# Order of the last two experts, of their last weights and of the tiles' norm, and the first expert's turn, on one Trainium2 core

## The chip, the cores and the metric

One core of a Trainium2 chip runs one launch. The metric is the device time of that launch in microseconds. The engines are TensorE (PE), VectorE (DVE), ScalarE (ACT), GpSimd (POOL) and SyncE (SP), whose queue issues most of the loads and stores.

## The reference, cut to what matters

Two transformer blocks run one after the other on 1024 tokens of width 1024, in float32. The change touches the last part of the second block, the mixture of 16 experts and the norm behind it:

```python
def expert_choice_moe(h, w_router, w_gate, w_up, w_down):
    cap = CAPACITY_FACTOR * T // N_EXPERTS            # 128 tokens for each expert
    gate, idx = lax.top_k(jnp.swapaxes(affinity, 1, 2), cap)
    xe = jax.vmap(lambda hb, ib: hb[ib])(h, idx)
    a = jnp.einsum('becd,edf->becf', xe, w_gate)      # each weight 1024 x 1024
    u = jnp.einsum('becd,edf->becf', xe, w_up)
    ye = jnp.einsum('becf,efd->becd', jax.nn.silu(a) * u, w_down) * gate[..., None]
    # combine: out[idx] += ye
...
x = x + g2 * expert_choice_moe(hx2, ...)
return rmsnorm(x, final_norm_g)
```

## The kernel before, in words

All engines run their own list of instructions, written out by hand in order; they meet at semaphores. `x.did(name, key)` counts an event, `x.wait_ge(name, key)` waits for it.

**Weights.** The 16 experts have 48 matrices, cut into 192 weights of 256 rows by 1024 columns (1 MB), numbered n in the order in which TensorE uses them (`EW`, `moe_order`, L3609). SP loads weight n into one of eleven places (`e_load`), once the weight eleven before is split. ScalarE rounds it to float32r, the high part (`e_high`), once the weight four before is used up, as there are four pairs of places for high and low parts. VectorE subtracts to get the low part, the rest (`e_low`). TensorE makes each float32 product of three float32r matmuls: high by high, high by low, low by high (`mm3`, L411). One weight (k index 0 and 1, column halves c of 512) is 12 matmuls, in two groups of six.

**An expert e.** TensorE does the gate product (gate e), the up product, the turn of the next expert's tokens (`turn_x`, 8 transposes), the down product of the expert before (down e-1), and the turn of the hidden row (`turn_h`, 8 transposes). ScalarE applies silu to the gate; VectorE multiplies it with up into `hb` (events `eu_out`, one for each half). After a turn ScalarE rounds (`xe_high`, `hb_high`) and VectorE subtracts (`xe_low`, `hb_low`). VectorE scales the down product into `yt`; GpSimd scatters it with an add into `xa_dram` (event `sc_st`), and gathers the tokens for the experts ahead.

**The end.** In expert 15 the order is gate 15, down 14, up 15, `turn_h` 15, down 15. The tokens of expert 15 are not scattered. When scatter 14 has landed, SP reads back `xa_dram` as eight tiles `XF[i]`, and GpSimd gathers the 128 rows of expert 15 (`rows`). ScalarE squares and sums each tile, VectorE forms mean and inverse root with ScalarE's root between them, scales the tiles (`y_out_f`) and SP stores them. `last_rows(c)` (L3934) adds half c of down 15 to `rows`; then `rows` has its own norm, and GpSimd writes these rows over the stored tiles, last of all.

**Queues around the change.** TensorE waits for the low part of each weight, in the order of the weights. In `moe_act` (L3817) and `moe_dve` (L3839) each product brings four roundings and four rests for the weights three to six ahead of its first, and then the product's own work (silu, `hb`, `yt`).

## Time and profile before

| what | value |
|---|---|
| median of 3 runs | 2835.88 us (2834.59 to 2837.06) |
| the profiled execution | 2833.19 us |
| its span | 2831.4 us |
| busy: PE, DVE, ACT, POOL | 2728.4, 2013.1, 1312.0, 555.9 us |
| experts, first transpose to the last matmul | about 2248 to 2812 us |
| end of the span behind the last matmul | 19 us |

Times in the rows are us from the span's start. A row of the timeline has the start, the length, the engine, the line and operation, what is written and read, how many instructions are merged into it, and in brackets how long the engine sat idle before it and what ended that. Matmul ends are modelled and overlap the next one's start, so a group's length over its count is the pace. L132 is any matmul, L135 any transpose, L138 any activation, L141 any `tensor_tensor`, L147 any `scalar_tensor_tensor`; shapes tell them apart: 128x2048 is a weight, 128x1024 a tile, 128x512 half a tile or a turned half.

### The profile page before, as it was taken

To read this page: it belongs to the slowest core of one execution; us is meant where nothing else is said; L and a number is where in the kernel's file an instruction comes from. 1 tells how busy PE (TensorE), PEld (TensorE's weight loads), DVE (VectorE), ACT (ScalarE), POOL (GpSimd) and SP (SyncE) were. 2 spreads that over 40 slices of the span, in tenths; PEclk is the share of its full clock that TensorE was granted. 3 is DMA by queue.
4 is the path that set the end of the run, shared out by engine and by line. 5 is a ranking of instruction groups with operands and counts; after the bars stand their busy time and mean duration, and the time that the engine had idled before them with its cause. 6 is when DMAs were issued, how large, how long until landed. Compare 5 with 4: busy or idle time off the path is not lost.

```text
span 2831.4 us, 35182 instructions
## 1 busy us (share of the span) xinstructions
PE 2728.4 (96%) x13692; PEld 2186.4 (77%) x13692; DVE 2013.1 (71%) x2776; ACT 1312.0 (46%) x2035; POOL 555.9 (20%) x499
## 2 busy tenths in 40 slices
PE   7999999999999999999999999999999399999996
PEld 6777778788778888988888876666788288888885
DVE  5344455888885788787866656665665689999997
ACT  4344534333332455433222355454323277777775
POOL 0011111655455011511111121111100300100000
PEclk9999999999999999999999999999999699999998
DMA  4110123445552997233222260111763699999996
GB/s 151 51 46 31 45 77 110 123 123 160 177 169 68 381 282 218 79 101 111 83 82 74 106 193 31 45 38 38 219 217 144 233 362 396 395 397 396 396 396 234
DMA packets 270617, 494.11 MB, mean 175 GB/s; under 512 B 30124, under 2 KB 141892, under 8 KB 269940
## 3 DMA queue, kind: packets, MB, share of 16 engines
q1 hardware_dynamic: 240864, 396.40, 40.2%
q0 software_dynamic: 29440, 95.43, 10.5%
q8 instruction: 109, 1.79, 0.3%
q14 instruction: 56, 0.46, 0.1%
q10 hardware_dynamic: 148, 0.04, 0.0%
HBM read 424.60 MB, written 67.21 MB: 174 GB/s over the span
## 4 chain that ended last, share of the span: by engine, by line
PE 87%; DVE 6%; ACT 2%; DMA 2%; issue 2%; POOL 1%; POOLq 0%; SPq 0%; DVEq 0%; ACTq 0%
PE PS L132 81%; PE PS L135 6%; DVE m L141 3%; ACT m L138 1%; DVE m L147 1%; POOL m L141 1%; DMA x_scratch<-m 1%; DVE m L183 0%; DVE m L186 0%; DVE m L180 0%; DMA m<-x_scratch 0%; ACT L138 0%; DVE m L150 0%; DMA m<-pc_scratch 0%; DMA m<-in_x_dram 0%
## 5 line engine op out<-in xcount | busy, mean ns | idle before, releaser
L132 PE MATMUL PS<-m,m 128*128 128x512 f32 (+6 forms) x11818 | 2526.8, 388 | 20.1 <-DVE m L141 10.3
L132 PEld LDWEIGHTS PS<-m,m 128*128 128x128 f32 (+2 forms) x11818 | 1987.8, 184 | 495.0 <-issue 90.6
L138 ACT ACTIVATE m<-m 128x512 fp32r<-128x512 f32 (+5 forms) x893 | 811.7, 930 | 877.1 <-PE PS L132 386.0
L141 DVE TENSOR_TENSOR m<-m,m 128x512 fp32r<-128x512 f32 (+5 forms) x920 | 1024.8, 1143 | 218.1 <-ACT m L138 199.6
L138 ACT ACTIVATE m<-PS 128x512 f32<-128x512 f32 (+3 forms) x497 | 276.9, 582 | 482.4 <-PE PS L135 288.7
L141 DVE TENSOR_TENSOR m<-PS,m 128x512 f32<-128x512 f32 (+1 forms) x456 | 300.1, 684 | 193.0 <-PE PS L132 136.7
L141 POOL TENSOR_TENSOR m<-m,m 128x512 f32<-128x512 f32 (+4 forms) x176 | 273.4, 1557 | 598.6 <-DVE m L141 260.0
L135 PE MATMUL PS<-ident,m 128*128 128x128 f32 x1650 | 230.7, 278 | 63.0 <-DVE m L156 36.0
L135 PEld LDWEIGHTS PS<-ident,m 128*128 128x128 f32 x1650 | 188.0, 141 | 111.8 <-DVE m L156 36.3
L138 ACT ACTIVATE m<-m,small 128x640 f32<-128x640 f32 (+4 forms) x200 | 156.1, 785 | 84.9 <-DVE small L150 84.6
L156 DVE COPY m<-PS 128x512 f32<-128x512 f32 (+2 forms) x160 | 97.1, 609 | 114.4 <-PE PS L135 87.4
L147 DVE SCALAR_TENSOR_TENSOR m<-m,small,m 128x512 f32<-128x512 f32 (+1 forms) x154 | 163.8, 1088 | 7.1 <-DMA m<-x_scratch 3.7
L150 DVE CUSTOM_DVE_ANT_0 m<-PS,m,small 128x640 f32<-128x640 f32 (+1 forms) x128 | 103.7, 847 | 63.4 <-PE PS L132 63.3
L147 DVE SCALAR_TENSOR_TENSOR m<-m,vecT,m 128x512 fp32r<-128x512 f32 (+3 forms) x96 | 63.4, 716 | 53.4 <-ACT m L138 52.8
L141 POOL TENSOR_TENSOR m<-m 128x512 f32<-128x512 f32 x62 | 85.2, 1382 | 29.7 <-DMA m<-in_w_gate_up_dram 17.5
L141 POOL TENSOR_TENSOR m<-ident,small 128x1024 f32<-128x1024 f32 x16 | 30.3, 1892 | 260.0 <-DVE small L162 260.0
L150 DVE CUSTOM_DVE_ANT_0 m<-PS,m 128x1024 f32<-128x1024 f32 (+7 forms) x64 | 45.8, 754 | 49.3 <-PE PS L132 49.3
L195 POOL DMA_INDIRECT m<-xh_scratch,small x16 | 20.2, 1264 | 300.0 <-PE PS L135 258.5
L141 DVE TENSOR_TENSOR m<-m,PS 128x512 f32<-128x512 f32 x75 | 50.8, 685 | 31.3 <-PE PS L132 31.2
L195 POOL DMA_INDIRECT xa_scratch<-m,small x15 | 25.6, 1709 | 216.7 <-DVE m L147 216.7
L138 ACT ACTIVATE m<-m,vecT 128x512 fp32r<-128x512 f32 (+2 forms) x80 | 41.2, 601 | 44.3 <-PE PS L132 44.3
L141 DVE TENSOR_TENSOR m<-m 128x512 f32<-128x512 f32 (+1 forms) x57 | 40.7, 714 | 0.1
(89 smaller groups left out, 495.8 us busy)
## 6 DMA issues: line engine op xcount, KB each, us to landing
m<-in_w_exp_gate_dram SPq DMA_DIRECT2D x64, 1024.0 KB, 8.1
m<-in_w_exp_up_dram SPq DMA_DIRECT2D x64, 1024.0 KB, 8.5
m<-in_w_exp_down_dram SPq DMA_DIRECT2D x64, 1024.0 KB, 7.7
m<-in_w_mod_dram SPq DMA_DIRECT2D x48, 512.0 KB, 3.7
m<-in_w_gate_up_dram SPq DMA_DIRECT2D x44, 512.0 KB, 6.4
m<-in_w_in_dram SPq DMA_DIRECT2D x21, 1024.0 KB, 5.1
m<-in_w_in_dram SPq DMA_DIRECT2D x25, 512.0 KB, 5.2
x_scratch<-m POOLq DMA_DIRECT2D x24, 512.0 KB, 4.3
```

Of the source, the lines that this page charges most:

```text
L132: return Unsent() if self.e is None else self.e.matmul(o, l, r, start=first, stop=last, **k)
L135: return Unsent() if self.e is None else self.e.transpose(o, i, ident)
L138: return Unsent() if self.e is None else self.e.activation(o, i, fn, **k)
L141: return Unsent() if self.e is None else self.e.tensor_tensor(o, a, b, op)
L147: return Unsent() if self.e is None else self.e.scalar_tensor_tensor(out=o, in0=a, scalar=s, in1=b, op0=op0, op1=op1)
L150: return Unsent() if self.e is None else self.e.tensor_tensor_reduce(**k)
L156: return Unsent() if self.e is None else self.e.tensor_copy(o, i)
L195: return Unsent() if self.e is None else self.e.indirect_dma_start(*a, **k)
```

## The change

- **First turn.** `turn_h` of expert 0 goes behind gate 1 on all engines. Gate 0 waits for the low half that each of its weights needs, no longer for both at the start.
- **Order of the end.** gate 14, down 13, up 14, then the turns `h(14, 0)`, `x(15)`, `h(14, 4)`, then down 14, gate 15, up 15, down 15. The order of loads follows.
- **Groups of up 14, up 15.** The six-matmul groups run so that column half 0 is done before half 1; `hb`'s first half is turned within up 15, its second within down 15.
- **Last two weights.** 190 and 191 are no longer split: `last_product` multiplies the raw float32 weight with the float32 turned row (`hb_turned_late`).
- **Norm of the tiles.** The squares of tiles 0 to 3, the table load for the root and the first scaling move from `final_act` and `final_dve` into up 15. `rows`' first half is multiplied by the gain ahead, and is scaled by ScalarE beside VectorE's second half.

```diff
-            if e_ == 15:
-                steps = [("gate", 15), ("down", 14), ("up", 15), ("turn_h", 15), ("down", 15)]
+            if e_ == 0:
+                steps = [("gate", 0), ("up", 0), ("turn_x", 1)]
+            elif e_ == 1:
+                steps = [("gate", 1), ("turn_h", 0), ("up", 1), ("turn_x", 2), ("down", 0), ("turn_h", 1)]
+            elif e_ == 14:
+                steps = [("gate", 14), ("down", 13), ("up", 14), ("down", 14)]
+            elif e_ == 15:
+                steps = [("gate", 15), ("up", 15), ("down", 15)]
...
+        hb_turned_late = ar(118, 4, 128)
+        BY_TILE = [(kg, c) for kg in range(4) for c in range(2)]
+        UP_14 = [(0, 0), (1, 0), (2, 0), (0, 1), (1, 1), (3, 0), (2, 1), (3, 1)]
+        UP_15 = [(0, 0), (1, 0), (2, 0), (0, 1), (3, 0), (1, 1), (2, 1), (3, 1)]
+        DOWN_15 = [(0, 0), (0, 1), (1, 0), (1, 1), (2, 0), (3, 0), (2, 1), (3, 1)]
...
+            order = {("up", 14): UP_14, ("up", 15): UP_15, ("down", 15): DOWN_15}.get((what, e), BY_TILE)
+            for kg, c in order:
+                if what == "gate" and e == 0:
+                    pe.wait_ge("xe_low", e, kg // 2 * 4)
+                if what == "down" and e >= 14 and (e, kg // 2) != (15, 1):
+                    pe.wait_ge("hb_low", e, kg // 2 * 4)
+                if (what, e) == ("down", 15) and kg >= 2:
+                    last_product(pe, n + kg, banks[c], kg, c)
+                    continue
...
+                if (what, e, kg, c) == ("up", 15, 1, 1):
+                    turn_h_pe(pe, 15, 0)
+                elif (what, e, kg, c) == ("down", 15, 0, 1):
+                    turn_h_pe(pe, 15, 4)
...
+        def last_product(pe, n, b, kg, c):
+            pe.wait_ge(e_names[n % NR], "e", n)
+            pe.wait_ge("hb_high", 15, 4)
+            for k in range(2):
+                t = pe.matmul(PS[:, b, :], hb_turned_late[:, 2 * kg + k - 4, :], e_raw(n)[:, k, half512(c)], False, kg + k == 4)
...
+                    if e == 14:                     # moe_pe, behind up 14
+                        turn_h_pe(pe, 14, 0)
+                        turn_x_pe(pe, 15)
+                        turn_h_pe(pe, 14, 4)
...
+                if (what, e) == ("up", 14):         # moe_act
+                    for n_ in range(n + 3, n + 6):
+                        e_high(act, n_)
+                    hb_round(act, 14, 0)
+                    e_high(act, n + 6)
+                    hb_round(act, 14, 4)
+                    e_high(act, n + 7)
+                    turn_x_act(act, 15)
...
+                elif (what, e) == ("up", 15):
+                    act.wait_ge("eg_out", 15, 1)
+                    act.activation(tab, one, ACT.Sqrt).then_inc(*act.did("act_table"))
+                    e_high(act, n + 3)
+                    final_square(act, 0)
+                    final_square(act, 1)
+                    e_high(act, n + 4)
+                    hb_round(act, 15, 0)
+                    e_high(act, n + 5)
+                    root_of(act, ssum[:, 0:2], "f", 0)
+                    final_square(act, 2)
+                    final_square(act, 3)
...
+                if (what, e) == ("up", 14):         # moe_dve
+                    e_low(dve, n + 3)
+                    e_low(dve, n + 4)
+                    hidden(dve, 14, 0)
+                    hidden(dve, 14, 1)
+                    hb_rest(dve, 14, 0)
+                    e_low(dve, n + 5)
+                    hb_rest(dve, 14, 4)
+                    e_low(dve, n + 6)
+                    e_low(dve, n + 7)
+                    turn_x_dve(dve, 15)
...
+                elif (what, e) == ("up", 15):
+                    e_low(dve, n + 3)
+                    hidden(dve, 15, 0)
+                    e_low(dve, n + 4)
+                    hb_rest(dve, 15, 0)
+                    final_mean(dve, 0)
+                    hidden(dve, 15, 1)
+                    e_low(dve, n + 5)
+                    final_scale(dve, 0)
...
         def final_dve(dve):
+            final_mean(dve, 1)
+            final_scale(dve, 1)
+            final_mean(dve, 2)
+            final_scale(dve, 2)
+            last_rows(dve, 0)
+            final_mean(dve, 3)
+            dve.wait_ge("act_junk~", "r", 0)
+            dve.tensor_scalar(ssr[:, 0:1], ssr[:, 0:1], 1.0 / 1024, EPS, ALU.mult, ALU.add).then_inc(*dve.did("dve_order~"))
+            dve.tensor_tensor(rows[:, 0:512], rows[:, 0:512], fg[:, 0:512], ALU.mult).then_inc(*dve.did("row_sum", "gain"))
+            final_scale(dve, 3)
             last_rows(dve, 1)
```

## Rows read from the trace of the kernel before

**Rows 1.** The page, busy time of each engine: us, share of the span, instructions.
```profile
PE 2728.4 (96%) x13692; PEld 2186.4 (77%) x13692; DVE 2013.1 (71%) x2776; ACT 1312.0 (46%) x2035; POOL 555.9 (20%) x499
```
**Rows 2.** Stretch: window, length, busy (count) of PE, PEld, DVE, ACT, POOL; clock, DMA.
```profile
2600.00:2700.00 100.00, 100.00 (x467) 83.26 (x466) 92.41 (x60) 75.27 (x54) 8.76 (x6) 1.00 1.03 400
```
**Rows 3.** Timeline of the end, with `down 15`, `last_rows(1)` and the last scaling.
```profile
2797.55 1.25 PE L135 MATMUL PS<-ident,m 128*128 128x128 f32 x8 [1.76 <-DVE m L141]
...
2799.71 12.74 PE L132 MATMUL PS<-m,m 128*128 128x512 f32 x48 [0.91 <-DVE m L141]
...
2818.66 0.74 DVE L147 SCALAR_TENSOR_TENSOR m<-PS,small,m 128x512 f32<-128x512 f32 x1
...
2820.92 0.16 DVE L141 TENSOR_TENSOR small<-small 128x1 f32<-128x1 f32 x1 [0.79 <-ACT m L138]
...
2821.74 1.28 DVE L147 SCALAR_TENSOR_TENSOR m<-m,small,m 128x1024 f32<-128x1024 f32 x1
```
**Rows 4.** Stretch, VectorE alone: window, length, busy (count), clock, DMA share, GB/s.
```profile
2741.44:2818.66 77.22, 68.37 (x53) 0.97 0.80 297
```
**Rows 5.** Stretches, TensorE alone; the first number behind the count is the granted clock.
```profile
2252.00:2256.00 4.00, 4.00 (x10) 0.50 0.41 131
2277.40:2281.00 3.60, 1.85 (x11) 1.00 1.03 416
2795.80:2799.70 3.90, 1.25 (x8) 1.00 0.72 254
2799.93:2803.35 3.42, 3.42 (x9) 0.50 0.90 328
```
**Rows 6.** Timeline between `up 0` and `gate 1`.
```profile
2276.18 1.04 PE L135 MATMUL PS<-ident,m 128*128 128x128 f32 x8
...
2277.87 3.67 DVE L141 TENSOR_TENSOR m<-PS,m 128x512 f32<-128x512 f32 x6
...
2278.61 1.26 PE L135 MATMUL PS<-ident,m 128*128 128x128 f32 x8 [1.39 <-DVE m L141]
...
2280.41 22.07 PE L132 MATMUL PS<-m,m 128*128 128x512 f32 x96 [0.54 <-DVE m L141]
```
**Rows 7.** Timeline of TensorE: float32 products of L1144; a turn, three products behind it.
```profile
379.58 6.83 PE L132 MATMUL PS<-m,m 128*128 128x512 f32 x16
...
2762.07 1.04 PE L135 MATMUL PS<-ident,m 128*128 128x128 f32 x8
...
2762.87 32.93 PE L132 MATMUL PS<-m,m 128*128 128x512 f32 x144
```
**Rows 8.** Timeline at the start of `gate 0`.
```profile
2250.11 0.69 DVE L141 TENSOR_TENSOR m<-PS,m 128x512 fp32r<-128x512 f32 x1 [6.88 <-ACT m L138]
...
2251.71 24.64 PE L132 MATMUL PS<-m,m 128*128 128x512 f32 x96 [1.41 <-DVE m L141]
```
**Rows 9.** Groups of 2741.44 to 2818.66 by form: the rests on VectorE, mean ns.
```profile
L141 DVE TENSOR_TENSOR m<-m,m 128x2048 fp32r<-128x2048 f32 x21 | 47.6, 2290 | 5.5 <-ACT m L138 5.3
```
**Rows 10.** Timeline: two rests, a rounding, the table load.
```profile
2742.05 4.59 DVE L141 TENSOR_TENSOR m<-m,m 128x2048 fp32r<-128x2048 f32 x2 [0.85 <-ACT m L138]
...
2765.97 1.92 ACT L138 ACTIVATE m<-m 128x2048 fp32r<-128x2048 f32 x1 [0.37 <-PE PS L132]
...
2801.25 1.28 ACT L138 ACT_TABLE_LOAD   x1
```
**Rows 11.** Timeline of GpSimd: scatter 14.
```profile
2788.13 3.35 POOL L195 DMA_INDIRECT xa_scratch<-m,small  x1 [21.11 <-DVE m L147]
```
**Rows 12.** Tile `xa_scratch`, 2300 to 2760: scatters 0 to 12, us to landing.
```profile
L195 POOL DMA_INDIRECT xa_scratch<-m,small x13: 1591/1591/1627, 2317.5 to 2731.0; - x13
...
DMA to landing us min/median/max: 8.3/9.0/9.8
```
**Rows 13.** DMA issues, 2785 to 2800: scatter 14, us to landing.
```profile
xa_scratch<-m,small POOLq DMA_INDIRECT x1, 7.8
```
**Rows 14.** SP's loads of the tiles, 2795 to 2800, us to landing.
```profile
DMA to landing us min/median/max: 3.3/8.6/11.3
```

More of the change, by code:

```diff
@@ L3758, in expert_product @@
                 bank_of["e_acc", what, e, c] = banks[c]
-            last = (what, e) == ("down", 15)
-            for kg, c in [(0, 0), (0, 1), (1, 0), (1, 1), (2, 0), (3, 0), (2, 1), (3, 1)] if last else [
-                    (kg, c) for kg in range(4) for c in range(2)]:
+            order = {("up", 14): UP_14, ("up", 15): UP_15, ("down", 15): DOWN_15}.get((what, e), BY_TILE)
[7 more added lines that the diff above has]
+                    continue
                 H, L = e_split(n + kg)
                 pe.wait_ge(*e_low_of(n + kg))
-                if last:
-                    pe.wait_ge("hb_low", e, kg // 2 * 4)
                 for k in range(2):
@@ L3783, in moe_pe @@
                 if what == "gate":
-                    pe.wait_ge("xe_low", e, 4)
+                    if e:
+                        pe.wait_ge("xe_low", e, 4)
                     expert_product(pe, n, (xeh, xel), "gate", e, "eg_out")
@@ L3819, in moe_act @@
             for what, e, n in moe_order:
-                if n is not None:
+                if (what, e) == ("up", 14):
[6 more added lines that the diff above has]
+                    turn_x_act(act, 15)
+                elif (what, e) == ("down", 14):
+                    for n_ in range(n + 4, n + 7):
+                        e_high(act, n_)
+                elif (what, e) == ("up", 15):
+                    act.wait_ge("eg_out", 15, 1)
+                    act.wait_ge("masks", "one")
+                    act.activation(tab, one, ACT.Sqrt).then_inc(*act.did("act_table"))
[8 more added lines that the diff above has]
+                    final_square(act, 3)
+                elif (what, e) == ("down", 15):
+                    hb_round(act, 15, 4)
+                elif n is not None:
                     for n_ in range(n, n + 4):
@@ L3841, in moe_dve @@
             for what, e, n in moe_order:
-                if n is not None:
+                if (what, e) == ("up", 14):
[9 more added lines that the diff above has]
+                    turn_x_dve(dve, 15)
+                elif (what, e) == ("down", 14):
+                    for n_ in range(n + 4, n + 7):
+                        e_low(dve, n_)
+                elif (what, e) == ("up", 15):
[7 more added lines that the diff above has]
+                    final_scale(dve, 0)
+                elif n is not None:
                     for n_ in range(n, n + 4):
-                        if n_ and n_ + 3 != 191:
+                        if n_:
                             e_low(dve, n_ + 3)
-                if what == "up":
+                if what == "up" and e < 14:
                     for c in range(2):
-                        dve.wait_ge("e_out", "up", e, c)
-                        dve.wait_ge("eg_out", e, c)
-                        if e:
-                            dve.wait_ge("hb_turned", e - 1, 4)
-                        dve.tensor_tensor(hb[:, half512(c)], ps("e_acc", "up", e, c), sil[c], ALU.mult).then_inc(*dve.did("eu_out", e, c))
+                        hidden(dve, e, c)
                 elif what == "turn_x" and e < 16:
@@ L3871, in moe_dve, with hidden, hb_rest @@
                                                  g2row[:, half512(c)], ALU.mult, ALU.mult).then_inc(*dve.did("ey_out", e, c))
+        def hidden(dve, e, c):
+            dve.wait_ge("e_out", "up", e, c)
+            dve.wait_ge("eg_out", e, c)
+            if e:
+                dve.wait_ge("hb_turned", e - 1, 4)
+            dve.tensor_tensor(hb[:, half512(c)], ps("e_acc", "up", e, c), sil[c], ALU.mult).then_inc(*dve.did("eu_out", e, c))
+        def hb_rest(dve, e, k0):
+            dve.wait_ge("hb_high", e, k0)
+            dve.tensor_tensor(hbl[:, k0:k0 + 4, :], turned("hb_turned", e, k0), hbh[:, k0:k0 + 4, :].bitcast(F32),
+                              ALU.subtract).then_inc(*dve.did("hb_low", e, k0))
         def gather(pool, e):
@@ L3918, in final_sp, with final_square @@
             sp.wait_ge("sc_st", "out")
+        def final_square(act, i):
+            act.wait_ge(f"x_in{i}", "f")
+            square(act, XF[i], ssum[:, i:i + 1], "f", i, junk=xf_junk)
         def final_act(act):
-            act.wait_ge("masks", "one")
-            act.activation(tab, one, ACT.Sqrt).then_inc(*act.did("act_table"))
-            for j in range(4):
-                for i in (2 * j, 2 * j + 1):
-                    act.wait_ge(f"x_in{i}", "f")
-                    square(act, XF[i], ssum[:, i:i + 1], "f", i, junk=xf_junk)
+            root_of(act, ssum[:, 2:4], "f", 1)
+            for j in (2, 3):
+                final_square(act, 2 * j)
+                final_square(act, 2 * j + 1)
                 root_of(act, ssum[:, 2 * j:2 * j + 2], "f", j)
@@ L3931, in final_act @@
                 square(act, rows[:, half512(c)], ssr[:, c:c + 1], "r", c, junk=row_junk[:, half512(c)])
-            root_of(act, ssr[:, 0:1], "r")
+            root_of(act, ssr[:, 1:2], "r")
+            act.wait_ge("row_sum", "gain")
+            act.wait_ge("rstd", "r")
+            act.activation(rows[:, 0:512], rows[:, 0:512], ACT.Copy, scale=rsr[:, 0:1]).then_inc(*act.did("rows_out"))
         def last_rows(dve, c):
```

74 lines of the change are left out of this document (35 added, 39 removed).

## The prediction
> **What bounds the kernel now.** I read the page's busy lines first: TensorE is busy 96% of the span [rows 1]. The stretches by stage say more. In the middle of the experts TensorE is busy for all of its 100 us and VectorE for 92.4 of them [rows 2], so TensorE sets the pace and VectorE has 8% to spare. Then I read the two places that the change touches, in order of time.
>
> At the end the bound is VectorE. TensorE's last 48 matmuls start at 2799.71 and are over at 2812.45; `last_rows(1)`, which waits for them, starts at 2818.66 [rows 3], 6.2 us later, because VectorE still works through the scaling of the eight tiles. From 2741.44 (the last moment at which both kernels have done the same) to 2818.66 VectorE is busy 68.37 of 77.22 us, so idle 8.85 [rows 4]. What TensorE loses near 2797 (1.76 and 0.91 us idle, then a clock of 0.50) is hidden under that [rows 3, 5].
>
> At the first expert TensorE is the bound. Its last up matmuls end near 2276.2, then eight transposes, 1.39 us idle, eight transposes, 0.54 us idle, and gate 1 at 2280.41 [rows 6]. Six VectorE operations of 0.61 us start at 2277.87: two products for `hb`, two rests `xe_low(1)`, two `hb_low(0)`. The fourth ends near 2280.3, and that is what gate 1 waits for, not the turn of `hb`.
>
> **The first turn: costs.** Gate 1 still waits for `xe_low(1, 4)`. VectorE still does both products first, and reaches them when rest 10 is done, which hangs on TensorE's up product. So gate 1 starts no sooner; the 3.4 us after the x turn become one idle stretch, and the eight transposes of `hb(0)`, which were free in it, now stand between gate 1 and up 1, where TensorE is the bound: 2762.87 - 2762.07 = 0.80 us [rows 7]. +0.80.
>
> Gate 0 by halves: its first half may start when the first rest is done, 2250.11 + 0.69 = 2250.80, where it now starts at 2251.71 [rows 8], 0.85 us sooner. The clock there is 0.50 [rows 5], so if it rises at the same moment the 0.85 is worth half, 0.43; if the slow stretch moves along, 0.85. I take 0.65. All that follows hangs on TensorE's own ends, so it passes on. -0.65.
>
> The clock at gate 1. Two gaps in the expert stage resemble the new one. From the last up matmul to gate 1, now 4.2 us with sixteen transposes in it, the clock stayed at 1.00. From the last up matmul to down 15, 3.9 us with eight transposes, it was 1.00 and then 0.50 for 3.42 us [rows 5]. The new gap is 4.2 us with eight transposes, so nearer the second. A fall costs 3.42 us at half speed: eight matmuls at 0.427 instead of 0.227, +1.6. Bounds 0 and 1.6; I take the fall.
>
> **The end: TensorE's own sum.** Two weights go unsplit: 24 matmuls of 0.227 (144 in 32.93 less the last one's tail) become 8 of float32. The eight float32 products at 379.58 (sixteen records, two each) take 6.83, so 0.854 each [rows 7]: 6.83 - 5.45 = +1.4. Gate 14 starts one expert (144 x 0.227 and two turns, 34.3) before gate 15's 2762.87, at 2728.5. From there the work is 312 x 0.227 + 6.83 + three turns of 0.80 = 80.1, with its end near 2808.7 if nothing waits. The Trainium skill (FP8 and Floating Point Precision, TensorE Precision Notes) says that true FP32 takes four passes; by that a product would cost 4 x 0.227 = 0.908 and the edit +1.8. The row decides for 0.854, and under VectorE's queue neither counts.
>
> **The end: VectorE's work.** Off: two rests of 2.24 (4.48; 2.29 alone, less the overlap [rows 9, 10]) and one `hb_low` of 0.64 (0.69 alone, as in [rows 8]). On: the gain of the first half of `rows`, 0.69, and one small operation, 0.17. 68.37 - 5.12 + 0.86 = 64.1.
>
> **VectorE's waits, walked through.** Rounding to high part 1.92, which starts 0.37 after a weight's last matmul; rest 2.24 behind it [rows 10].
> - before 2750 as now: three waits, the first 0.85 [rows 10], together 1.7
> - up 14 by halves holds weight 172 until its fourth group of six matmuls (1.363 each), 2750.36 + 5.45 = 2755.8, so rounding 176 ends at 2758.1 and VectorE idles 2.3
> - `hidden(14, 1)` waits for TensorE, `hb_rest(14, 0)` for ScalarE: 0.9. Down 14 starts at 2763.2, gate 15 at 2774.1, up 15 at 2785.0; up 15 wants weights 185 and 186 early (1.36 and 2.7 us after its start) while rests 185 and 186 end at 2786.5 and 2788.7, so TensorE loses 1.2
> - rounding 187 stands behind two silus and the table load (1.28) [rows 10]: 0.7
> - `hidden(15, 0)` waits for up 15's fifth group, some 2793.4: 1.8
> - rest 188. On ScalarE rounding 188 stands behind squares 0 and 1, which wait for tiles read back after scatter 14. VectorE writes `yt(14)` until 2779.8; the scatter is issued at 2780.15, lands 8.3 later (7.8 on an empty queue, 8.3 to 9.8 beside the weights) [rows 11 to 13]; tile 0 comes 3.3 behind it [rows 14]: 2791.8. Squares until 2794.2, rounding until 2796.1, rest 188 then: 2.2
> - four roots at 0.24, and 0.65 before the new small operation: 1.6
>
> Sum 11.2 idle against 8.85. 64.1 + 11.2 = 75.3, so `last_rows(1)` at 2816.7, 1.9 sooner. TensorE is done at 2812.4, under it. Behind `last_rows(1)` one sum goes (0.16 and a step of 0.04) and the last scaling is of 512 columns (0.70 for 1.28) [rows 3]: -0.8, with ScalarE's half beside it. End: -2.7.
>
> Against this scatter speaks a rule of the Trainium skill (SBUF — State Buffer, "SBUF: two separate sides", the "DVE blocks DMA" trap): the descriptors of a GpSimd DMA cannot be written while VectorE runs an operation in a two-port mode. Here one scatter took 3.35 us on GpSimd instead of 1.59 [rows 11, 12], with VectorE busy; by the rule it may again, and the end would gain 1.8 less. Thirteen others took 1.6 beside the same work, so I take 1.6.
>
> **Sum.** -0.65 + 0.80 + 1.6 - 2.7 = -0.95. The profiled execution took 2833.19 (span 2831.4), so 2832.2 for its like; the median of the runs is 2835.88, 2.7 above it, and the difference is carried to that: 2834.9.
>
> **Rivals.**
> - The clock stays up at gate 1. For: the gap of equal length that didn't drop it. Against: half the transposes. -2.55, 2833.3.
> - The end is not held by the new waits. If the four large ones (2.3, 0.7, 1.8, 2.2) fell away, `last_rows(1)` would start at 2809.7, just behind TensorE's 2808.7, and the end would give 9.7; half of it is 6.2. With 0.15 at the first turn: -9.6 to -6.0, 2826.3 to 2829.9, say 2828. For: my walk chains some twenty steps. Against: each wait hangs on a slot or a landing that the order fixes.
> - Slower: the tiles come late. Square 0 stands ahead of rounding 188, the turn of `hb(15)` and rounding 189 on ScalarE. From 2788.3 on each us by which the squares are late costs one; I have them 3.5 late. Landings of such loads and scatters range from 3.3 to 11.3 [rows 12 to 14]: a scatter of 11.3 is +3, and tile 1 at 11.3 instead of a good us after tile 0 +6.8, in all -0.95 + 9.8, 2844.7. Above no change from tile 1 about 1 us later than I have it. Against: weight loads are over by then, so queues are short.
> - The turn behind gate 1 does not do what it says: that is in the sum, as it removes no wait.
>
> **Chances.** The forecast 0.43, the clock staying 0.31, the end freed 0.13, late tiles 0.08, others within 0.2% 0.05. Range: down to 2829.5 for half of the freed end, up to 2840 for tiles 5 us late; beyond lie about 0.1 below and 0.08 above. A measurement here tells 0.2% (5.7 us) from no change; below 2830.2 is faster: 0.15 with what the first case may reach; above 2841.5 slower: 0.08; same 0.77.
>
> **What would show it.** Gate 1's first matmul still released by VectorE, 4.2 us after up 0, and the clock in the stretch behind it. Eight transposes between gate 1 and up 1. Idle of VectorE of about 2.3 before rest 176 and 2.2 before rest 188, the latter under ScalarE's wait for a tile. Scatter 14 issued near 2780, TensorE over near 2812, `last_rows(1)` near 2817, each less the shift of the first part. The prediction is wrong if `last_rows(1)` starts as soon as TensorE's last matmul ends, or if gate 1 starts sooner after up 0.

## The result and the profile after

| | kernel before | kernel after |
|---|---|---|
| median of 20 runs each | 2835.47 us (2831.38 to 2838.53) | 2840.24 us (2838.03 to 2843.52) |
| profiled execution, its span | 2833.19, 2831.4 | 2840.7, 2838.9 |
| ratio after / before | | 1.0017, 95% interval 1.0011 to 1.0023 |

The change costs 4.8 us, 0.17%. That is within the 0.2% taken for no change, but 5.3 us over the forecast and 0.2 over the end of the range. The two profiled executions differ by 7.5 us; that of before was 2.3 under its median. The steps below are those of the profiles.

**The first expert.** Timeline of TensorE and VectorE in the kernel after, against [rows 6, 8]:

```profile
2250.81 0.69 DVE L141 TENSOR_TENSOR m<-PS,m 128x512 fp32r<-128x512 f32 x1 [6.76 <-ACT m L138]
...
2251.55 0.79 PE L132 MATMUL PS<-m,m 128*128 128x512 f32 x1 [0.56 <-DVE m L141]
...
2276.22 1.04 PE L135 MATMUL PS<-ident,m 128*128 128x128 f32 x8
...
2277.91 2.48 DVE L141 TENSOR_TENSOR m<-PS,m 128x512 f32<-128x512 f32 x4
...
2280.44 12.81 PE L132 MATMUL PS<-m,m 128*128 128x512 f32 x48 [3.19 <-DVE m L141]
...
2293.09 1.03 PE L135 MATMUL PS<-ident,m 128*128 128x128 f32 x8
...
2293.88 11.15 PE L132 MATMUL PS<-m,m 128*128 128x512 f32 x48
```

Gate 0 starts 0.74 us behind the start of the first low half, where it took 1.60 [rows 8]: 0.86 sooner. Gate 1 still starts 4.22 us behind the first transpose of the turn of expert 1's tokens (4.23 before), released by VectorE behind four operations. The turn of `hb(0)` takes 0.79 between gate 1 and up 1. The clock, in stretches of TensorE alone (the first number behind the count is the granted clock):

```profile
2277.00:2281.40 4.40, 1.21 (x7) 1.00 1.03 364
2281.40:2284.81 3.41, 3.41 (x10) 0.50 0.96 388
...
2803.64:2813.88 10.24, 5.29 (x13) 0.50 0.66 270
```

It fell to 1.2 GHz for 3.41 us behind the gap, and gate 1's 48 matmuls took 12.81 us where up 1's take 11.15.

**The end.** All engines in the kernel after, timeline, with the stretch that answers to [rows 4] at the foot:

```profile
2756.22 3.37 POOL L195 DMA_INDIRECT xa_scratch<-m,small  x1 [21.06 <-DVE m L147]
...
2760.49 2.29 DVE L141 TENSOR_TENSOR m<-m,m 128x2048 fp32r<-128x2048 f32 x1 [2.35 <-ACT m L138]
...
2780.61 1.40 DVE L147 SCALAR_TENSOR_TENSOR m<-PS,small,m 128x512 f32<-128x512 f32 x2
2781.93 8.89 DVE L141 TENSOR_TENSOR m<-m,m 128x2048 fp32r<-128x2048 f32 x4
2782.29 9.95 POOL L195 DMA_INDIRECT xa_scratch<-m,small  x1 [22.70 <-DVE m L147]
...
2791.95 2.29 DVE L141 TENSOR_TENSOR m<-m,m 128x2048 fp32r<-128x2048 f32 x1 [1.14 <-ACT m L138]
...
2795.99 0.69 DVE L141 TENSOR_TENSOR m<-PS,m 128x512 f32<-128x512 f32 x1 [1.75 <-PE PS L132]
2796.93 5.24 SPq L189 DMA_DIRECT2D m<-xa_scratch  x8
...
2801.38 1.06 ACT L138 ACTIVATE m<-m 128x1024 f32<-128x1024 f32 x1 [9.46 <-DMA m<-xa_scratch]
...
2803.68 1.89 ACT L138 ACTIVATE m<-m 128x2048 fp32r<-128x2048 f32 x1
...
2805.60 2.29 DVE L141 TENSOR_TENSOR m<-m,m 128x2048 fp32r<-128x2048 f32 x1 [8.91 <-ACT m L138]
...
2808.59 5.44 PE L132 MATMUL PS<-m,m 128*128 128x512 f32 x12 [8.04 <-DVE m L141]
...
2814.22 9.85 PE L132 MATMUL PS<-m,m 128*128 128x512 f32 x28
...
2826.35 0.75 DVE L147 SCALAR_TENSOR_TENSOR m<-PS,small,m 128x512 f32<-128x512 f32 x1
```
```profile
2744.00:2826.35 82.35, 63.52 (x53) 0.94 0.75 279
```
```profile
xa_scratch<-m,small POOLq DMA_INDIRECT x1, 14.6
```

Read from below. `last_rows(1)` starts at 2826.35 instead of 2818.66 [rows 3]. VectorE did less work up to it (63.52 us for 68.37) but was idle for 18.83 instead of 8.85, and 8.91 of that is one wait, ahead of rest 188. It waits for ScalarE's rounding 188, which stands behind squares 0 and 1, and these wait for tiles that SP may load only when scatter 14 has landed. The scatter was issued at 2782.29 and took 9.95 us on GpSimd instead of 3.35 [rows 11], until 1.42 us behind the end of four rests in a row, and landed 14.6 us after its issue (the line of DMA issues; 7.8 before [rows 13]). TensorE meanwhile idles for 8.04 us and then runs down 15's first matmuls at half clock.

The chain of the difference: 2.57 us have come in when gate 14 starts (2728.41 before, now 2730.98; nearly all of it the turn's 0.79 and the 1.66 of the clock), the end takes 82.35 us for 77.22, +5.13, and the tail behind `last_rows(1)` 4.47 for 4.64, -0.17. The sum is 7.5.

### The profile page after: what moved, and what is told of

Read it like the earlier page. It is cut to its first block, busy times and chain, and to the rows that moved or that the text cites. A ratio compares the mean times of both kernels' runs of the same rounds, so it can differ in the third digit from the quotient of the medians.

```text
span 2838.9 us, 35162 instructions
## 1 busy us (share of the span) xinstructions
PE 2732.9 (96%) x13684; PEld 2186.8 (77%) x13684; DVE 2003.9 (71%) x2774; ACT 1308.1 (46%) x2034; POOL 564.6 (20%) x499
## 4 chain that ended last, share of the span: by engine, by line
PE 86%; DVE 6%; DMA 3%; issue 2%; ACT 2%; POOL 1%; SPq 0%; POOLq 0%; DVEq 0%; ACTq 0%
PE PS L132 80%; PE PS L135 6%; DVE m L141 4%; ACT m L138 1%; DVE m L147 1%; POOL m L141 1%; DMA x_scratch<-m 1%; DMA m<-x_scratch 1%; DMA xa_scratch<-m,small 1%; DVE m L183 0%; DMA m<-in_w_down_dram 0%; DVE m L186 0%; DVE m L180 0%; ACT L138 0%; DVE m L150 0%
## 5 line engine op out<-in xcount | busy, mean ns | idle before, releaser
L195 POOL DMA_INDIRECT xa_scratch<-m,small x15 | 34.0, 2270 | 206.9 <-DVE m L147 206.9
```

The lines of the kernel that those rows point to most:

```text
L195: return Unsent() if self.e is None else self.e.indirect_dma_start(*a, **k)
```

## The experiments

The theory after the result: scatter 14 (GpSimd's add of expert 14's rows into `xa_dram`) is held on GpSimd by the rests in a row, and square 0 ahead of rounding 188 passes the delay on to VectorE and TensorE. The rivals: the clock and the turn at the first expert carry the loss; the tiles are late by traffic; the new orders at the end lose it by themselves. All results in one table; each kernel stands beside the kernel before on the same chip, whose median is in the third column. "Scatter" is scatter 14's time on GpSimd, "landing" from its issue, "stretch" from gate 0's first matmul to GpSimd's last scatter, each of the profiled execution; the work ahead of gate 0 varies by 3 us and more between executions, so the stretch is the cleaner measure of one profile. It still holds chance: at 1.2 GHz gate 0 ran for 3.0 to 6.0 us of its start in the 18 profiles, whatever the order, worth up to 1.5 us. The ratio on record is not that of the two medians (in `pool_first` they lie furthest apart, 0.9999 beside -1.4 us); its interval is about 2.5 us to either side in the rows of eleven runs.

| kernel | median | before | difference | ratio, 95% interval | scatter | landing | stretch |
|---|---|---|---|---|---|---|---|
| before | | | | | 3.35 | 7.8 | 571.6 |
| after | 2840.24 | 2835.47 | +4.8 | 1.0017, 1.0011 to 1.0023 | 9.95 | 14.6 | 579.3 |
| pool_first | 2833.42 | 2834.81 | -1.4 | 0.9999, 0.9990 to 1.0008 | 1.55 | 8.3 | 570.8 |
| psum_between | 2832.84 | 2834.81 | -2.0 | 0.9992, 0.9983 to 1.0001 | 1.55 | 6.0 | 569.8 |
| psum_after_one | 2832.49 | 2835.77 | -3.3 | one run | 3.35 | 7.9 | 570.1 |
| norm_back | 2837.63 | 2835.77 | +1.9 | 1.0006, 0.9997 to 1.0015 | 12.15 | 16.7 | 574.7 |
| short_break | 2832.98 | 2835.30 | -2.3 | 0.9993, 0.9983 to 1.0002 | 3.35 | 7.9 | 570.0 |
| ready_late, ready_mid | 2840.36, 2840.69 | 2835.30 | +5.1, +5.4 | one run each | 9.95 | 14.5, 14.4 | 579.1, 578.0 |
| ready_03, ready_09 | 2840.64, 2838.66 | 2838.80 (one run) | +1.8, -0.1 | one run each | 9.95 | 14.5, 14.6 | 576.8, 576.7 |
| squares_behind | 2833.22 | 2834.81 | -1.6 | 0.9994, 0.9985 to 1.0003 | 9.95 | 14.9 | 572.5 |
| turn_undone | 2837.59 | 2834.81 | +2.8 | 1.0008, 0.9999 to 1.0017 | 9.95 | 14.5 | 575.4 |
| turn_alone | 2837.22 | 2835.50 | +1.7 | 1.0006, 0.9997 to 1.0015 | 3.35 | 9.1 | 573.6 |
| whole_alone | 2833.86 | 2835.50 | -1.6 | 0.9993, 0.9984 to 1.0002 | 3.35 | 8.0 | 571.3 |
| behind_and_undone | 2831.83 | 2835.50 | -3.7 | 0.9987, 0.9978 to 0.9996 | 9.95 | 14.7 | 569.3 |
| behind_undone_psum | 2830.93 | 2835.50 | -4.6 | 0.9983, 0.9974 to 0.9992 | 1.55 | 6.1 | 569.8 |
| rest_first | 2832.56 | 2835.77 | -3.2 | 0.9989, 0.9980 to 0.9998 | 9.95 | 14.6 | 570.1 |

**1. Give GpSimd a moment.** `pool_first` lets VectorE wait behind `yt(14)` until GpSimd has worked a small fill behind the scatter; `psum_between` puts two more scalings of the down product, which read PSUM, ahead of rest 183.

```diff
+                    if e == 14:                                  # pool_first, moe_dve behind yt
+                        dve.wait_ge("described")                 # GpSimd's memset behind the scatter
...
+                    if e == 14:                                  # psum_between, same place
+                        for c in range(2):
+                            dve.scalar_tensor_tensor(row_junk[:, half512(c)], ps("e_acc", "down", e, c), ...)
```

> The changed kernel with one wait more: before rest 183 VectorE waits for a small memset that stands behind scatter 14 on GpSimd. Theory 1 (VectorE's unbroken row of rests, each reading two SBUF operands, keeps GpSimd from writing the scatter's descriptors; the late landing then holds square 0 and with it rounding 188): the scatter takes 1.6 to 2 us on GpSimd instead of 9.95, lands 8 to 9.5 us after its issue instead of 14.6, and ScalarE's wait of 9.46 us before square 0 shrinks to 2 to 4 us. By the walk of the prediction with those numbers the end comes 5.7 us sooner: median near 2834.5. Theory 2 (the scatter is slow for its own sake, its DMA queue being full of weight loads): still about 10 us on GpSimd, and the added wait makes it slower, 2848.

> The changed kernel with two VectorE operations more between yt(14) and rest 183: the same scaling of down 14 out of PSUM again, into an unused place, 1.4 us in all. VectorE is as busy as before behind the scatter's issue, but its operations read one SBUF operand and one of PSUM, as the hb rests do that follow the scatters of experts 0 to 13. Theory 1 (it is the rests, with both operands in SBUF, that keep GpSimd out): the scatter takes about 1.6 us on GpSimd, and the end comes some 5.7 us sooner than the changed kernel's: 2834.5. Theory 1b (any busy VectorE keeps GpSimd out): 8 to 11 us on GpSimd and 2841.5 to 2842. Theory 2 (full queue): 10 us, 2841.5.

Timeline of the two, `pool_first` first:

```profile
2778.74 1.55 POOL L195 DMA_INDIRECT xa_scratch<-m,small  x1 [22.69 <-DVE m L147]
...
2779.72 0.69 POOL L165 MEMSET small<- 128x1 f32 x1
2780.44 8.90 DVE L141 TENSOR_TENSOR m<-m,m 128x2048 fp32r<-128x2048 f32 x4 [1.98 <-POOL small L165]
...
2790.31 1.06 ACT L138 ACTIVATE m<-m 128x1024 f32<-128x1024 f32 x1 [0.51 <-DMA m<-xa_scratch]
```
```profile
2777.84 2.72 DVE L147 SCALAR_TENSOR_TENSOR m<-PS,small,m 128x512 f32<-128x512 f32 x4
2779.52 1.55 POOL L195 DMA_INDIRECT xa_scratch<-m,small  x1 [22.70 <-DVE m L147]
...
2780.47 8.89 DVE L141 TENSOR_TENSOR m<-m,m 128x2048 fp32r<-128x2048 f32 x4
```

The scatter takes 1.55 us in both, and square 0 waits 0.51 in `pool_first` instead of 9.46. Their medians lie 1.4 and 2.0 us under the kernel before, neither clear of noise, where the kernel after lies 4.8 over it, which is. So the held scatter costs 6 to 7 us by the medians and 5 to 7 by the ratios, no less than the whole loss. In `pool_first` VectorE is idle for 1.98 us more, and the kernel is still faster than the kernel after. `psum_between` shows that being busy is not what matters: VectorE works through, with one operand in PSUM, and the scatter passes.

**2. Which boundary is enough.** `psum_after_one` has the same two scalings one rest later; `norm_back` puts the early norm back into `final_act` and `final_dve`, so that a fifth rest follows without a break; `short_break` lets rest 184, the second of the four, wait for the rounding of weight 185.

```diff
+                        if (what, e, n_) == ("gate", 15, n + 1):  # short_break, ahead of rest 184
+                            dve.wait_ge("e_high", n + 5)
```

> The changed kernel with the same two PSUM-reading operations, but behind rest 183 instead of ahead of it; one look at the profile. If a rest with both operands in SBUF keeps GpSimd out for its length, and the operations with one operand in PSUM let it in, the scatter takes the 1.9 us that are left of rest 183 and then the 1.4 that it needed after the break in the changed kernel's profile: 3.3 to 3.5 us on GpSimd, where it took 9.95 with four rests in a row and 1.55 with the two operations first. If something other than the kind of operation decided (the queue of loads), it stays near 10 or near 1.6.

> The changed kernel with the early part of the norm put back: the table load, squares 0 to 3 and the first scaling stand behind down 15's roundings and rests again. Nothing in up 15 or down 15 waits for the tiles, though scatter 14 still takes 8 to 10 us on GpSimd. By my walk TensorE's 8 us gap goes, but all eight scalings now come behind the last rest: 2.8 us sooner than the changed kernel, 2837.4, and 2.5 to 5 us slower than with the squares merely moved behind the roundings. Rival (the early norm is worth nothing, only its place cost): as good as the squares moved, 2833 to 2834.

> The kernel after, with one wait more: rest 184, the second of the four behind yt(14), waits also for ScalarE's rounding of weight 185, which ended 0.34 us behind rest 183 in the kernel after. So VectorE is idle for 0.3 to 0.5 us after the first of the four rests. If one short idle moment is enough for GpSimd: scatter 14 takes 3.35 us on GpSimd (0.36 behind the start of rest 183 until 1.42 behind its end), lands 8 us after its issue, square 0 comes 6 us sooner, and the time is that of the version with the two PSUM operations behind rest 183 (2832.5) plus 0 to 1: 2833 to 2834.5. If the hold goes by what follows the break: 9.95 us and 2840.

Timelines of the three, in this order, the third in two fences:

```profile
2782.16 2.28 DVE L141 TENSOR_TENSOR m<-m,m 128x2048 fp32r<-128x2048 f32 x1
2782.52 3.35 POOL L195 DMA_INDIRECT xa_scratch<-m,small  x1 [22.69 <-DVE m L147]
...
2784.36 1.40 DVE L147 SCALAR_TENSOR_TENSOR m<-PS,small,m 128x512 f32<-128x512 f32 x2
```
```profile
2782.26 11.09 DVE L141 TENSOR_TENSOR m<-m,m 128x2048 fp32r<-128x2048 f32 x5
2782.62 12.15 POOL L195 DMA_INDIRECT xa_scratch<-m,small  x1 [22.70 <-DVE m L147]
```
```profile
2782.55 2.28 DVE L141 TENSOR_TENSOR m<-m,m 128x2048 fp32r<-128x2048 f32 x1
2785.17 6.70 DVE L141 TENSOR_TENSOR m<-m,m 128x2048 fp32r<-128x2048 f32 x3 [0.35 <-ACT m L138]
```
```profile
2782.90 3.35 POOL L195 DMA_INDIRECT xa_scratch<-m,small  x1 [22.70 <-DVE m L147]
```

One rest ahead of the opening gives 3.35 us, four 9.95, five 12.15: each further rest adds its 2.20, and the end lies 1.42 to 1.43 us behind the end of the last rest in each. An idle moment of 0.35 us is opening enough: this one wait turns +4.8 into -2.3 and leaves all else as it was. In `norm_back` the scatter is held longest, yet its median is 2.9 us better than that of the kernel after (+1.9 for +4.8), as expected, though the intervals overlap: without squares in the way of rounding 188 the late tiles cost less, as experiment 4 shows by itself.

**3. Why it got in before.** In the kernel before four rests follow `yt(14)` as well, yet the scatter took 3.35. Timeline of ScalarE and VectorE there:

```profile
2787.73 1.92 ACT L138 ACTIVATE m<-m 128x2048 fp32r<-128x2048 f32 x1 [0.80 <-PE PS L132]
```
```profile
2787.77 9.12 DVE L141 TENSOR_TENSOR m<-m,m 128x2048 fp32r<-128x2048 f32 x4
```

The row is 0.23 us longer than the 8.89 of the kernel after. It has an idle moment of 0.14 us, but behind the second rest, near 2792.3, when the scatter had been over since 2791.48 [rows 11]; it got in behind the first rest, without one. The second rest's rounding ended at 2789.65, 0.32 us before that rest began; in the kernel after all had been ready for 1.2 us and more. Four kernels made rest 184 ready later by a mark in gate 15's matmuls.

```diff
+                    if (what, e, kg, c, k) == ("gate", 15, KG, 0, K):   # late: KG 1, K 1; mid: 1, 0; 03: 2, 1; 09: 2, 0
+                        t.then_inc(*pe.did("g_mark"))
...
+                        if (what, e, n_) == ("gate", 15, n + 1):
+                            dve.wait_ge("g_mark")
```

> The kernel after, with rest 184 waiting also for the group of six matmuls in gate 15 that I place at 2783.6 plus a step of 0.3 (k index 1, column half 0), so that it becomes ready 0.2 to 0.4 us before rest 183 ends, without an idle moment of VectorE. In the kernel before, and in turn_alone and whole_alone, the second rest's rounding ended 0.32 us before its start each time, and GpSimd got in there; in the kernel after the second, third and fourth had been ready for over 1.2 us. If GpSimd gets in where the next rest became ready only while the last one ran: 3.35 us on GpSimd. If only an idle moment or an operand in PSUM lets it in: 9.95, and what let it in in the kernel before is something else.

> As ready_late, with the mark half a group (0.68 us) sooner, so that rest 184 is ready 0.9 to 1.1 us before rest 183 ends. If becoming ready while the last rest runs is enough: 3.35 us on GpSimd. If it has to be within the last few tenths, or if readiness doesn't count: 9.95.

> Gate 15 starts at 2776.84 (48 matmuls of down 14 behind 2765.94), so the marks of ready_late and ready_mid were passed before rest 183 began, and their wait was met at once. Here the mark is the end of gate 15's group with k index 2, column half 0, at 2776.84 + 5 x 1.363 = 2783.65, with a step of 0.3: rest 184 becomes ready at 2783.95, while rest 183 runs, 0.2 us ahead of the start that it had. If GpSimd gets in where the next rest only becomes ready while the last one runs (as in the kernel before): 3.35 us on GpSimd, without an idle moment of VectorE. If an idle moment is needed: 9.95.

> As ready_03 with the mark half a group (0.68 us) sooner: rest 184 ready at about 2783.3, 0.9 us ahead of its start. If any moment while rest 183 runs is enough: 3.35 us on GpSimd. If it has to be in the last few tenths, or an idle moment is needed: 9.95.

In the first two I had placed gate 15 a weight too late, and the mark had passed before rest 183 began; they only show that one wait more does nothing. In the other two the mark fell inside rest 183 (0.3 us ahead of that rest's end in `ready_03`, 1.0 in `ready_09`), with no idle moment. Timeline of VectorE in `ready_03`, four rests in a row again:

```profile
2782.98 8.89 DVE L141 TENSOR_TENSOR m<-m,m 128x2048 fp32r<-128x2048 f32 x4
```

The scatter took 9.95 us in all four (the times of single runs say nothing beyond that). So late readiness is not what opened the boundary before. ScalarE, idle at that boundary, is not it either. ScalarE in `norm_back`, the rounding for its fifth rest:

```profile
2788.85 1.91 ACT L138 ACTIVATE m<-m 128x2048 fp32r<-128x2048 f32 x1
```

It ended at 2790.76, so at the fourth boundary ScalarE was idle from 0.39 us ahead of the rest's end (0.40 before), and the fifth rest had been ready for 0.30 us when it began. That is the kernel before in both respects, and the boundary stayed closed. What differs otherwise is which weights' places the rests read and write (187 and 188 before, 183 to 186 after); that was not tried, and the cause stays open.

**4. The queue behind the tiles.** `squares_behind` puts squares 0 and 1 behind rounding 188, the turn's rounding and rounding 189.

```diff
                     e_high(act, n + 3)
-                    final_square(act, 0)
-                    final_square(act, 1)
                     e_high(act, n + 4)
                     hb_round(act, 15, 0)
                     e_high(act, n + 5)
+                    final_square(act, 0)
+                    final_square(act, 1)
```

with the first `final_mean` on VectorE behind rest 189.

> The changed kernel with squares 0 and 1 moved behind rounding 188, the turned half of hb(15) and rounding 189 on ScalarE, and with the first mean behind rest 189 on VectorE; the scatter is left as it is. Theory 1: GpSimd still takes 8 to 10 us for scatter 14 and the tiles still land near 2801, but nothing of the matrix products waits for them: TensorE's gap of 8.04 us before down 15 falls to under 1.5, and the end comes 5.4 us sooner by the walk, 2834.8. Rival (the tiles' landing sets the end through the eight scalings whatever stands ahead of them): 1 to 2 us sooner at most, 2838.5 or more.

From +4.8 to -1.6. The scatter still took 9.95 us and the tiles came as late; the largest gap of TensorE is 2.18 us instead of 8.04, and `last_rows(1)` starts at 2818.88:

```profile
2799.47 1.06 ACT L138 ACTIVATE m<-m 128x1024 f32<-128x1024 f32 x1 [0.20 <-DMA m<-xa_scratch]
...
2807.77 4.53 PE L132 MATMUL PS<-m,m 128*128 128x512 f32 x10 [2.18 <-ACT m L138]
```

So the loss needs both links of the chain: open the scatter, or keep the roundings from standing behind the tiles, and about 6 us are back.

**5. The first turn.** `turn_undone` is the kernel after with the turn of `hb(0)` in its old place (gate 0 by halves kept); `turn_alone` is the kernel before with only the turn behind gate 1. The diff is the first one of the change (the lists for experts 0 and 1), taken out or put in.

> The changed kernel with the turn of hb(0) back in its old place, ahead of gate 1; gate 0 keeps its two halves. By the prediction the move costs 0.80 for the turn and 1.6 for the fall of the clock (0.50 for 3.4 us behind gate 1's start in the changed kernel's profile): 2.4 us sooner, 2837.8, and the clock stays at 1.00 behind gate 1. Rival (the fall of the clock belongs to the earlier start of gate 0 or to chance): only 0.8 sooner, 2839.4. Rival (the turn's move gains): 2841 or more.

> The kernel before with one part of the change alone: the turn of hb(0) behind gate 1 (gate 0 still waits for both rests). My theory: gate 1 is still released by xe_low(1, 4) at the same distance behind up 0 (4.2 us), in one idle stretch of about 3.2 us, and the eight transposes stand between gate 1 and up 1: +0.8. The clock falls to 0.50 behind gate 1's start more often than in the kernel before: up to +1.6. Together +0.8 to +2.4: median 2835.6 to 2837.2 where before has 2834.8. Rival (the move is what it was meant for): 0.5 to 2 us faster than before.

Put in alone the turn costs 1.7 us in the median, and taken out of the kernel after it gives 2.0 back (+2.8 for +4.8). Both agree with 0.8 and a part of the clock's 1.6, but neither is clear of noise by itself: the interval of `turn_alone` holds no change, and that of `turn_undone` overlaps that of the kernel after. What the profiles show without noise is the 0.79 between gate 1 and up 1. Timeline of TensorE in `turn_alone`:

```profile
2276.40 1.04 PE L135 MATMUL PS<-ident,m 128*128 128x128 f32 x8
2280.63 12.64 PE L132 MATMUL PS<-m,m 128*128 128x512 f32 x48 [3.19 <-DVE m L141]
2293.11 1.03 PE L135 MATMUL PS<-ident,m 128*128 128x128 f32 x8
```

The gap is one stretch and the turn stands in TensorE's way. The clock fell from 2280.34 to 2283.75. It is no clean part of the price: with the turn behind gate 1 it fell there in all 13 profiles (after and twelve experiments), with the turn in its old place in three of five (`whole_alone`, `behind_undone_psum` and, against what I expected of it, `turn_undone`; not in before and `behind_and_undone`). The fall may be likelier with the change, and a part of its cost is paid before too; how large a part, five profiles can't tell.

**6. The last two weights unsplit, alone.** `whole_alone` is the kernel before with 190 and 191 multiplied raw.

> The kernel before with one part alone: weights 190 and 191 unsplit, as float32 products. VectorE loses two rests (4.5 us) and one hb rest; TensorE's product is 1.4 longer, under VectorE's queue. My walk of the old order without them: the eight tiles' squares and scalings become bound by the landing of the tiles behind scatter 14, so of 5.1 us only 1.2 come off the end: 2833.6. Rival (VectorE's work alone sets the end): 4 to 5 us faster than before, 2830. Rival (TensorE's longer products count): 2836.

-1.6, with an interval that just holds no change. Timeline of VectorE ahead of the first mean and root:

```profile
2805.39 0.17 DVE L144 TENSOR_SCALAR small<-small 128x2 f32<-128x2 f32 x1 [4.34 <-ACT m L138]
```

The 4.5 us that the two rests took become waits for the tiles' squares: 4.34 us here, where it was 1.58 in the kernel before, and 1.77 ahead of the second mean, where there was none. Whether the edit pays in full where the tiles come sooner was not run.

**7. Together.** `behind_and_undone` joins `squares_behind` and `turn_undone`; `behind_undone_psum` adds the two scalings of `psum_between`. `rest_first` is `squares_behind` with `xe_low(1)` ahead of the products of `hb(0)` on VectorE and GpSimd's last waits in another order.

```diff
-                if what == "up" and e < 14:
+                if what == "up" and 0 < e < 14:
...
                     turn_x_dve(dve, e)
+                    if e == 1:
+                        for c in range(2):
+                            hidden(dve, 0, c)
...
-            pool.wait_ge("y_out_f", "rows")
-            pool.wait_ge("rows_out")
             pool.wait_ge("out_st")
+            pool.wait_ge("rows_out")
+            pool.wait_ge("y_out_f", "rows")
```

> The changed kernel with two of the repairs at once: squares 0 and 1 behind the roundings, and the turn of hb(0) in its old place, with gate 0 in halves kept. If the two gains (7.0 and 2.7 us against the changed kernel) come from different places they add: 2833.2 - 2.65 = 2830.6, 4 us faster than before. If they share a cause, 2833.

> The same with the two PSUM-reading operations between yt(14) and rest 183 as well, so that scatter 14 gets its descriptors out at once. With the squares no longer ahead of the roundings the landing of the tiles should matter little: VectorE pays 1.4 us for the two operations, and gains back what it waits for tile 3 (1.5 us in the profile with the squares behind). Expected within 1 us of the kernel without them, 2830 to 2831.5. If the landing still held the end it would be 3 us faster, 2828.

> The kernel with the squares moved behind the roundings, and two small edits: at the first expert VectorE makes the two rests xe_low(1) ahead of the two products for hb(0), with the turn of hb(0) behind gate 1 as in the change; and GpSimd's last wait is the one for VectorE's half of the rows, with the waits for the stores and for ScalarE's half ahead of it. In the change gate 1 waits for rests that stand behind products which it doesn't need. Expected: gate 1's first matmul 1.2 to 1.3 us closer to up 0 (2.9 instead of 4.2 us), 0.5 us less between VectorE's last scaling and the last scatter (0.28 instead of 0.78), so 1.7 us sooner than with the squares moved, 2831.5, and up to 1.6 more where the shorter gap spares the fall of the clock: 2830 to 2831.5. Rival: the products, now later, hold something else and nothing is gained, 2833.

All three beat both kernels, their intervals lying under 1, by less than 0.2% of the time; the best median is 4.6 us under that of the kernel before. In `rest_first` gate 1 starts 1.2 us sooner, as expected, but the clock fell all the same, and the other order of the waits gained nothing: GpSimd's last scatter still starts 0.84 us behind VectorE's last operation.

The chain that ended last shows why. Its pieces ahead of the last scatter in before, after and `rest_first`, a fence each:

```profile
2821.51 0.02 POOLq L115
2821.53 1.53 issue
```
```profile
2829.29 0.73 ACT m L138
2830.02 0.03 POOLq L115
2830.05 0.54 issue
```
```profile
2821.56 0.04 POOLq L115
2821.60 0.54 issue
```

GpSimd's queue has an instruction of its own for waits (POOLq L115) ahead of the scatter, and the scatter itself carries one wait more; the semaphores in the traces tell which. In the kernel before the first held only the wait for the tiles' stores and was over 1.5 us ahead of VectorE's scaling; the scatter carried the wait for that scaling and started 0.28 us behind it. In the kernel after the first also holds the wait for ScalarE's half of `rows`, is over at 2830.05, and the scatter starts 0.77 us behind it. In `rest_first` the first holds the waits for both halves, and the one for the stores has gone into the scatter, so that edit could gain nothing. In `turn_alone`, with the old waits, the stores landed late; the wait instruction ended 0.06 us ahead of VectorE's scaling, and there too the scatter starts 0.76 us behind it. Of the 18 profiles 16 have that step of 0.76 to 0.77; in before and `whole_alone`, where the wait instruction ended over half a microsecond ahead of the scaling, the scatter starts 0.28 us behind the scaling.

## Why the prediction was wrong, point by point

**The step that failed: the price of scatter 14.** I took 1.6 us on GpSimd and 8.3 to landing, as "thirteen others took 1.6 beside the same work". It took 9.95 and 14.6, so the landing came 6.3 us later behind the issue; the tiles took 1.1 more again, and the wait ahead of rest 188 grew from my 2.2 to 8.91. The others had not stood beside the same work. Behind the `yt` of scatters 0 to 13 VectorE had two `hb_low`, which read PSUM; I looked at how busy VectorE was, not at what its operands were. The only row of the old order with nothing but rests behind `yt` was the one of 3.35 us [rows 11], and I had it in hand as the odd one. Scatter 13, which the change also moves ahead of a rest, took 3.37 and cost nothing, as nobody waited.

The rule of the Trainium skill that I weighed against this edit and set aside (SBUF — State Buffer, "SBUF: two separate sides") had the direction right and my price for it, 1.8, was far too low. What I cited of it speaks of two-port modes, and no run shows that the rests run in one. By the same section the ports that VectorE and GpSimd share are held by one of them for a whole instruction, and an operation of VectorE with both inputs in SBUF takes them too, against a GpSimd operation that reads SBUF. The rests have both inputs in SBUF, the scalings in `psum_between` have not, and 9.95 against 1.55 agrees, if the scatter counts as an operation that reads SBUF, which no run shows by itself. "For a whole instruction" does not: here four and five in a row held it, and one boundary of the same kind did not.

**The rival "the tiles come late" is what happened**, with its chain (square 0 ahead of rounding 188, the turn of `hb(15)` and rounding 189 on ScalarE) and its rate of one for one; `squares_behind` shows the chain. I gave it 0.08, because I let only the landing vary and not the time on GpSimd. The wait measured 6.7 over mine, which lies within its price of up to 9.8.

**The rest of the end's sum held.** VectorE's work: 64.1 forecast, 63.52. The waits: 2.3 ahead of rest 176, 2.35; 0.9 at `hidden(14, 1)` and `hb_rest`, 0.93; 0.7 ahead of rest 187, 1.14; 1.8 at `hidden(15, 0)`, 1.75. The 2.2 ahead of rest 188 was too much even for an open scatter: in the four profiles of the new order that have one and the squares in their place it is 0 to 1.09. The price of TensorE's float32 products was not read. Of the tail's -0.8 only -0.17 came: its operations got shorter, but GpSimd's last scatter starts 0.78 us behind VectorE's last one instead of 0.28. That term was mis-sized: ScalarE's half shortened the scaling by 0.53 (0.75 for 1.28), but put a late wait into GpSimd's wait instruction, at a price of 0.5 (experiment 7).

With the scatter open the sum comes near: from gate 0's first matmul to the last scatter my terms are +0.2 (the slow clock that moves along), +0.8, +1.6 and -2.7, so -0.1. `pool_first` has -0.8 there and `psum_between` -1.8 (its scatter landed 6.0 us after the issue, not 8.3). Of that 0.6 and 0.8 are luck, as less of gate 0 lay in the slow clock than in the profile of before (from gate 0 to the turn 23.87 and 23.65 us for 24.48). The medians are 1.4 and 2.0 below before where I forecast 0.95, which noise of 2.5 us neither supports nor refutes.

**The first expert held in what VectorE and the turn do.** Gate 0 starts 0.86 sooner, for my 0.85. What the clock takes of that is not shown: from gate 0 to the turn it took 24.66 us after 24.48, which would leave 0.68 for my 0.65, but over the 18 profiles it took 23.3 to 24.7 with no order in it, so that agreement is luck. Gate 0 by halves was not timed alone. The turn cost 0.79 for 0.80. The clock fell, and 48 matmuls took 1.66 us more for my 1.6; charging all of that to the change was too much, as it also fell in three of the five profiles with the old order. `turn_alone` gives +1.7 in the median, between my 0.80 and 2.4.

**The unsplit weights** gave -1.6 alone, an interval that just holds no change; their gain in the new order was not run by itself.

**The rivals on the fast side.** "The clock stays" did not come in any profile of the new order. "The end is freed" did not either: even with the scatter at 1.55 VectorE waits 1.75 us at `hidden(15, 0)` for TensorE's group.

## What to carry to other kernels

Before a DMA that GpSimd issues is put ahead of a chain that others wait for, read what VectorE does right behind it: a row of operations with both operands in SBUF can hold it to the row's end, and a wait of a third of a microsecond, or two operations on PSUM, behind the first lets it through. And a transfer's consumer should not stand ahead of work in an engine's queue that doesn't need the transfer: moving two squares behind three roundings left the same late landing without a measurable price (-1.6 us, beside -1.4 with the scatter open).

At a join of several waits in GpSimd's queue, read which wait the last instruction carries itself: splitting the last scaling between two engines saved 0.53 us there and cost 0.5 again in the wait.

A price that all rows but one agree on is that of their neighbourhood; look at the neighbours of the odd one first, above all where the change copies them.

## What the runs showed of the hardware that I had not expected

- An indirect scatter of GpSimd took 1.55 to 1.63 us on the engine with VectorE on PSUM operands or idle behind it, 3.35 to 3.37 with one subtraction of 128x2048 from SBUF to SBUF begun first, 9.95 with four in a row, 12.15 with five. Where it was held it ended 1.42 to 1.45 us behind the end of the last operation that held it.
- VectorE's operations in a row, each starting 0.08 us before the last one ends, kept GpSimd out over their boundaries in ten profiles, and let it in at the first boundary in the three with the old order at the end (before, `turn_alone`, `whole_alone`). Readiness of the next operation and ScalarE's idleness at that moment are ruled out as the reason, alone and together; the reason is not known.
- An idle moment of VectorE of 0.35 us was worth about 7 us in the launch (+4.8 to -2.3 in the medians).
- GpSimd's last scatter started 0.28 us behind the end of VectorE's last operation where it carried that wait itself and the others were met well before (before, `whole_alone`), and 0.76 to 0.77 us behind the end of the separate wait instruction in the other sixteen profiles, where that ended 0.06 us ahead of VectorE's last operation or later.
